# Stick-breaking softplus on whole tiles with its own table set, and the modulation product in 256-column blocks

## The reference, cut to what matters

```
log_1m = where(earlier, log_sigmoid(-z), 0)
between = cumsum(log_1m, reverse) - log_1m
att = where(earlier, exp(log_sigmoid(z) + between), 0)
```

```
mod = silu(c) @ w_ada + b_ada        # [1,1024] @ [1024,3072], twice
shift, scale, gate = split(mod, 3)
```

## Time and profile before

| | |
|---|---|
| median of 3 runs | 1934.13 us (1929.14 to 1935.0) |
| the profiled execution's own time | 1935.0 us |
| its span, first to last instruction | 1932.9 us |
| PE busy | 1817.4 us, 94% |
| DVE, ACT, POOL busy | 1263.3, 1029.7, 146.0 us |
| mean granted TensorE clock | 0.974 |
| HBM read | 284.06 MB |

### The profile page before, as it was taken

The page is one execution under the profiler, slowest core; times in us unless marked ns, Lnnn a source line. Parts: engine busy times, 40 slices in busy tenths (PEclk is TensorE's granted clock), DMA queues, the critical chain, the costliest instruction groups (busy, mean ns, idle before and its releaser), DMA issues.

```text
span 1932.9 us, 43768 instructions
## 1 busy us (share of the span) xinstructions
PE 1817.4 (94%) x18871; PEld 1631.5 (84%) x18871; DVE 1263.3 (65%) x1783; ACT 1029.7 (53%) x1585; POOL 146.0 (8%) x106
## 2 busy tenths in 40 slices
PE   6987999999989999898999999998899999998998
PEld 5887788889979888887698888887798888887887
DVE  6875367865436675486668856876467755775764
ACT  5834455554535554354655545744465554564455
POOL 0051100000000000014000000151100000000000
PEclk9999999999989999899899999999999999998999
DMA  6420145557576655355465562320245555443441
GB/s 190 132 86 4 53 146 184 190 182 244 174 233 217 197 191 180 110 174 178 150 198 184 186 204 93 120 76 4 68 153 191 178 188 169 134 146 104 152 132 66
DMA packets 288535, 287.92 MB, mean 149 GB/s; under 512 B 15240, under 2 KB 286456, under 8 KB 288344
## 3 DMA queue, kind: packets, MB, share of 16 engines
q1 hardware_dynamic: 285048, 284.02, 45.8%
q10 hardware_dynamic: 3296, 1.11, 0.3%
HBM read 284.06 MB, written 1.05 MB: 148 GB/s over the span
## 4 chain that ended last, share of the span: by engine, by line
PE 90%; DVE 4%; issue 3%; ACT 2%; DMA 0%; POOL 0%; SPq 0%; DVEq 0%; ACTq 0%; POOLq 0%
PE ps L419 23%; PE ps L420 12%; PE ps L401 10%; PE ps L403 9%; PE ps L402 9%; PE ps L814 3%; PE ps L436 2%; PE ps L437 2%; PE ps L438 2%; PE ps L713 1%; PE ps L784 1%; PE ps L798 1%; PE ps L675 1%; PE ps L641 1%; PE ps L727 1%
## 5 line engine op out<-in xcount | busy, mean ns | idle before, releaser
L463 DVE TENSOR_TENSOR wl<-raw,wh 128x1024 fp32r<-128x1024 f32 x484 | 596.5, 1251 | 345.4 <-ACT wh L453 340.9
L453 ACT ACTIVATE wh<-raw 128x1024 fp32r<-128x1024 f32 x484 | 499.4, 1041 | 432.0 <-PE ps L420 191.2
L419 PE MATMUL ps<-HH,wh 128*128 128x512 f32 x1408 | 489.7, 391 | 0.0
L420 PE MATMUL ps<-HH,wl 128*128 128x256 f32 x1408 | 397.0, 282 | 0.0
L419 PEld LDWEIGHTS ps<-HH,wh 128*128 128x128 f32 x1408 | 264.3, 188 | 55.6 <-issue 0.4
L401 PE MATMUL ps<-HH,wh 128*128 128x256 f32 x928 | 271.4, 292 | 10.2 <-DVE HH L2498 5.5
L420 PEld LDWEIGHTS ps<-HH,wl 128*128 128x128 f32 x1408 | 266.1, 189 | 0.1
L402 PE MATMUL ps<-HH,wh 128*128 128x256 f32 x928 | 263.6, 284 | 0.0
L403 PE MATMUL ps<-HH,wl 128*128 128x256 f32 x928 | 263.3, 284 | 0.0
L401 PEld LDWEIGHTS ps<-HH,wh 128*128 128x128 f32 x928 | 179.3, 193 | 20.8 <-issue 6.6
L402 PEld LDWEIGHTS ps<-HH,wh 128*128 128x128 f32 x928 | 179.6, 193 | 1.2 <-issue 1.2
(11 more groups left out here) (323 smaller groups left out, 3119.6 us busy)
## 6 DMA issues: line engine op xcount, KB each, us to landing
raw<-in_ffn_w_gu_dram SPq DMA_DIRECT2D x88, 1024.0 KB, 5.1
raw<-in_ffn_w_down_dram SPq DMA_DIRECT2D x32, 1024.0 KB, 5.1
raw<-in_w_in_dram SPq DMA_DIRECT2D x32, 1024.0 KB, 5.4
raw<-in_rw_w_rkv_dram SPq DMA_DIRECT2D x24, 1024.0 KB, 5.3
B<-in_w_ada_dram SPq DMA_DIRECT2D x24, 1024.0 KB, 7.7
raw<-in_ds_w_in_dram SPq DMA_DIRECT2D x14, 1024.0 KB, 5.3
raw<-in_ffn_w_down_dram SPq DMA_DIRECT2D x16, 768.0 KB, 4.4
raw<-in_sb_w_qkv_dram SPq DMA_DIRECT2D x12, 1024.0 KB, 5.5
```

The source lines that it names most:

```text
L419: e.matmul(o[:, m, :], h_[:, k, c], x_, start=k0 + k == 0, stop=False, skip_group_check=True)
L420: i = e.matmul(o[:, m, 0:S], l_[:, k, c], x_[:, 0, :], start=False, stop=k0 + k == kt - 1, skip_group_check=True)
L453: e.activation(wh[:, u % UNITS, 0:kn * 256], raw[:, j % RAW, k0 * 256:(k0 + kn) * 256], ACT.Copy).then_inc(*up("hi"))
L463: e.tensor_tensor(wl[:, u % UNITS, 0:kn * 256], raw[:, j % RAW, k0 * 256:(k0 + kn) * 256], wh[:, u % UNITS, 0:kn * 256].bitcast(F32), ALU. ...
```

## The change

Five things change.

1. `pe_ada` works block by block: 16 matmuls of 256 moving columns instead of 32 of 128; the eight k go to the four partition groups in turn, so the groups now hold partial sums over k. Each block signals its own end, and only its own load is waited for.
2. `act_ada` copies 128x512 instead of 128x128, and `pe_mod` adds the four groups and turns the result with four matmuls of one column instead of one of four.
3. On ACT, `softened` is cut in three: `sizes` (two Abs), `exps` (one Exp over 128x1536) and `logs` (a load of the table set `natural_log`, then one Ln over 128x1536). `weights` first loads the combined table set again. One `hi` now stands ahead of `sizes` and one between each of the parts. For g=3 `act_ada(2)` stands between `sizes` and `exps`.
4. On DVE, `soft(g)` stands behind q of the next group and one `lo`; it waits once for the single Ln.
5. In the feed-forward of layer 1, `dve_mod(6)` moves from i=7 to i=8.

```diff
-        add("sel", i[:, None] == 32 * np.arange(4)[None, :])
+        add("sel", (i % 32 == 0)[:, None])
...
         def pe_ada(e, t):
-            blocks = [2 * t, 2 * t + 1]
-            for i in blocks:
+            for u in range(2):
+                i = 2 * t + u
+                w = whole(KD, 256)(ada_slot[i])
                 e.wait_ge(s_ada[i % 4], 16 * (i // 4 + 1))
-            for k in range(KD):
-                for c in range(4):
-                    w = whole(KD, 256)(ada_slot[blocks[c // 2]])
-                    q = e.matmul(o[32 * c:32 * c + 32, 0:128], scb[:, k, :], w[:, k, c % 2 * P:c % 2 * P + P], ...)
-            q.then_inc(*up("mm", ("ada block", 2 * t), ("ada block", 2 * t + 1), ("ada", t)))
+                for k in range(KD):
+                    q = e.matmul(o[32 * (k % 4):32 * (k % 4) + 32, u * 256:u * 256 + 256], scb[:, k, :], w[:, k, :],
+                                 start=k < 4, stop=k >= 4, skip_group_check=True)
+                q.then_inc(*up("mm", ("ada block", i), *([("ada", t)] if u else [])))
...
         def pe_mod(e, t):
-            e.matmul(o[:, 0:4], ada_rows[:, 0:P], C("sel"), ...)
+            for m in range(4):
+                q = e.matmul(o[:, m:m + 1], ada_rows[:, m * P:m * P + P], C("sel"), ...)
...
         act_ada:
-            e.activation(ada_rows, PS("ada", t)[:, 0:P], ACT.Copy)
+            e.activation(ada_rows, PS("ada", t)[:, :], ACT.Copy)
...
         act_stickbreak:
-            def softened(g):    # 2 Abs, 2 Exp, 2 Ln of 128x768
+            def sizes(g):       # 2 Abs of 128x768
+            def exps(g):
+                e.activation(exw, exw, ACT.Exp, scale=-1.0)
+            def logs(g):
+                e.preload_act_table_set("natural_log")
+                e.activation(exw, exw, ACT.Ln, bias=1.0)
             def weights(g):
+                log_and_exp(e)
...
             for g in range(3):
-                softened(g)
-                hi(e)
+                hi(e, 1)
+                sizes(g)
+                hi(e, 1)
+                exps(g)
                 if g:
                     act_ada(e, g - 1)
-                hi(e)
+                hi(e, 1)
+                logs(g)
+                hi(e, 1)
                 weights(g)
                 hi(e)
-            softened(3)
+            sizes(3)
             act_ada(e, 2)
+            exps(3)
+            logs(3)
             act_ada(e, 3)
             act_ada(e, 4)
             weights(3)
...
         dve_ffn:
-                if layer == 1 and i == 7:
+                if layer == 1 and i == 8:
                     dve_mod(e, 6)
...
         dve_stickbreak:
             for g in range(3):
+                block("q", g + 1)
+                lo(e, 1)
                 soft(g)
-                block("q", g + 1)
+                lo(e, 1)
+                block("k", g + 1)
                 lo(e)
-                block("k", g + 1)
                 if g:
                     dve_mod(e, g - 1)
-                lo(e)
                 value_block(g + 1)
                 heads_out(g)
```

More of the change, by code:

```diff
@@ L517, in build @@
         ada_slot = [BUF[i] for i in (9, 10, 11, 9, 10, 11, 9, 10, 11, 2, 9, 10, 7, 9, 10, 7, 11, 14, 2, 11, 14, 2, 11, 14)]
-        ada_rows = BUF[12][:, 768:896]
+        ada_rows = BUF[12][:, 768:1280]
         def ada_load(e, i):
@@ L706, in pe_ada @@
                 e.wait_ge(*at("dve", "scb"))
-            blocks = [2 * t, 2 * t + 1]
-            for i in blocks:
+            for u in range(2):
+                i = 2 * t + u
+                w = whole(KD, 256)(ada_slot[i])
                 e.wait_ge(s_ada[i % 4], 16 * (i // 4 + 1))
-            for k in range(KD):
-                for c in range(4):
-                    w = whole(KD, 256)(ada_slot[blocks[c // 2]])
-                    q = e.matmul(o[32 * c:32 * c + 32, 0:128], scb[:, k, :], w[:, k, c % 2 * P:c % 2 * P + P],
-                                 start=k == 0, stop=k == KD - 1, skip_group_check=True)
-            q.then_inc(*up("mm", ("ada block", 2 * t), ("ada block", 2 * t + 1), ("ada", t)))
+                for k in range(KD):
+                    q = e.matmul(o[32 * (k % 4):32 * (k % 4) + 32, u * 256:u * 256 + 256], scb[:, k, :], w[:, k, :],
+                                 start=k < 4, stop=k >= 4, skip_group_check=True)
+                q.then_inc(*up("mm", ("ada block", i), *([("ada", t)] if u else [])))
         def pe_mod(e, t):
@@ L719, in pe_mod @@
             e.wait_ge(*at("act", ("ada", t)))
-            e.matmul(o[:, 0:4], ada_rows[:, 0:P], C("sel"), start=True, stop=True,
-                     skip_group_check=True).then_inc(*up("mm", ("mod", t)))
+            for m in range(4):
+                q = e.matmul(o[:, m:m + 1], ada_rows[:, m * P:m * P + P], C("sel"), start=True, stop=True, skip_group_check=True)
+            q.then_inc(*up("mm", ("mod", t)))
         def pe_to_tm(e, key, src, j):
@@ L1450, in act_ada @@
                 e.wait_ge(*at("mm", ("mod", t - 1)))
-            e.activation(ada_rows, PS("ada", t)[:, 0:P], ACT.Copy).then_inc(*up("act", ("ada", t)))
+            e.activation(ada_rows, PS("ada", t)[:, :], ACT.Copy).then_inc(*up("act", ("ada", t)))
         def act_ffn(e, layer):
@@ L1700, in act_stickbreak @@
             ex, at_ = sb_pairs(BUF[7]), sb_pairs(BUF[8])
-            def softened(g):
+            exw = BUF[7][:, 0:1536]
+            def sizes(g):
                 for r in range(2):
                     e.wait_ge(*at("mm", ("sb", "z", 2 * g + r)))
[L1705 to L1711, removed]
+                    i = e.activation(ex[r], PS2[r][:, :, 0:384], ACT.Abs)
+                i.then_inc(*up("act", ("sb", "abs", g)))
+            def exps(g):
+                e.wait_ge(*at("act", ("sb", "abs", g)))
+                e.activation(exw, exw, ACT.Exp, scale=-1.0).then_inc(*up("act", ("sb", "e", g)))
+            def logs(g):
+                e.preload_act_table_set("natural_log")
+                e.wait_ge(*at("act", ("sb", "e", g)))
+                e.activation(exw, exw, ACT.Ln, bias=1.0).then_inc(*up("act", ("sb", "l", g)))
             def weights(g):
+                log_and_exp(e)
                 for r in range(2):
@@ L2401, in soft @@
             def soft(g):
+                e.wait_ge(*at("act", ("sb", "l", g)))
                 for r in range(2):
-                    e.wait_ge(*at("act", ("sb", "l", 2 * g + r)))
                     e.scalar_tensor_tensor(out=sp_[r], in0=PS2[r][:, :, 0:384], scalar=0.0, in1=ex[r], op0=ALU.max,
```

## The result

The changed kernel takes 1954.39 us (median of 4 runs, 1952.05 to 1963.59) against 1934.57 before (4 runs). Over all runs of both kernels the ratio is 1.0136, 95% interval 1.0107 to 1.0165: 1.4% slower, or 26 us. Its 29 executions spread from 1950.6 to 1970.5. The profiled one took 1962.87, span 1960.7, mean clock 0.967. I had forecast slower by 17.6 (1943 to 1958); the direction held, the size did not: 1.0136 times 1934.1 is 1960.

What follows compares the result with a forecast made beforehand. PE was taken to bound the kernel, busy 94% of the span. The terms +7.1 +3.4 -3.5 +3.4 +4.8 +2.4 = +17.6 us on 1934.1 gave 1951.7 us, 0.9% slower, range 1943 to 1958.

Steps and rivals of the forecast that it cites:

- What bounds the kernel: Whole kernel: PE, busy 94% of the span; ACT and DVE work is free until PE waits for it.
- The waits before `sums`: Stick-breaking groups 0 to 2: PE waits 2.3, 2.4 and 2.4 us for ACT's longer chain, +7.1 us.
- the link named first: Stick-breaking groups on ACT: the `hi` ahead of `sizes` makes Abs run behind it, from 506.8 instead of 500.6.
- the rival that made it 1.4 longer: Stick-breaking table switch: each wait 1.4 longer, clock dropping every time; +23.5 us, 1957.6; chance 0.08.
- `pe_mod`: Modulation matmuls on PE: eight machine instructions at 0.07 us instead of two, +0.42 each; +3.4 outside the tail.
- `pe_ada`: Modulation matmuls on PE: half the instructions with twice the columns change nothing; 0, bounds -0.15 and +0.2 each.
- The tail: Stick-breaking stage's end: `act_ada(2)` comes earlier, so the output projection starts earlier; -3.5 us, longer `pe_mod` included.
- u(8): Feed-forward of layer 1: PE waits for the bank `dve_mod(6)` frees, +4.8 us, and +2.4 for the clock behind.
- The clock after the waits: Behind the three waits before `sums`: clock falls to half speed after two of three, +3.4 us, bounds 0 and 5.1.
- The sum: Whole kernel: all terms together +17.6 us on the median of 1934.1, giving 1951.7 us, 0.9% slower.

Runs made afterwards that it cites:

- experiment 9: Changed kernel with the first `hi` of each stick-breaking group moved from ahead of the Abs to behind the Exp; ratio to the kernel before 1.0142.
- 10: Changed kernel with each group's third `hi` moved behind `logs`, and `soft` ahead of both `lo` on DVE; ratio to the kernel before 1.0107.
- 3: Changed kernel without the eight table loads of the stick-breaking stage, Ln taken from the combined set; ratio to the kernel before 1.0066.
- experiment 5: Kernel before with only `pe_mod`'s one matmul of four columns split into four of one column; ratio to the kernel before 1.0045.
- experiment 6: Kernel before with the new `pe_ada`, `act_ada` and `pe_mod`, no order changed; ratio to the kernel before 1.0045.
- tail_only: Kernel before with `act_ada(2)` moved behind the two Abs of group 3, ahead of its Exp; ratio to the kernel before 0.9978.
- old_stick: Changed kernel with ACT's and DVE's order of the stick-breaking stage as in the kernel before, the rest changed; ratio to the kernel before 1.0088.
- ada_only: Same run as experiment 6: kernel before with the new `pe_ada`, `act_ada` and `pe_mod`, no order changed; ratio 1.0045.
- mod4: Same run as experiment 5: kernel before with only `pe_mod`'s matmul split into four of one column; ratio 1.0045.
- early_mod: Changed kernel with `dve_mod(g-1)` of the stick-breaking groups ahead of the two `lo` again; ratio to the kernel before 1.0113.
- third_behind: Same run as 10: changed kernel with each group's third `hi` behind `logs`, and `soft` ahead of both `lo`; ratio 1.0107.
- abs_first: Same run as experiment 9: changed kernel with each group's first `hi` moved behind the Exp; ratio 1.0142.
- experiment 1: Changed kernel with `dve_mod(6)` back at i=7 of the feed-forward; ratio to the kernel before 1.0095.
- experiment 8: The changed kernel measured once more, nothing altered, on the same chip as the other experiments; ratio to the kernel before 1.0145.

## Why the prediction was right in direction and short in size

- **What bounds the kernel.** Right for what the trace locates: it is waits of PE, instructions added to it, and PE at half clock.
- **The waits before `sums`.** Right in place and size: 3 x 2.20 = 6.6 for +7.1. Wrong in the link named first. I led the chain from the `hi` ahead of `sizes`; experiment 9 shows that it alone is innocent, and 10 and 3 that the third `hi` and the table load make the wait. My own sum had the third `hi`'s release in it, so the number came out right.
- **The table switch.** The load is 1.28 and the next ACTIVATE starts 1.30 after the load's start; the rival that made it 1.4 longer did not come, although its time, 1957.6, is the nearest to the result. The Trainium skill ("ScalarE: Activation LUTs", section "What ACT_TABLE_LOAD costs") adds a drain of about 1.38 us; no run here shows one: taking the load out shortened the waits by 1.42, of which 1.28 is the load. My text leaves most of this rival out of the range, yet its 1957.6 lies inside 1943 to 1958.
- **`values(2)`.** Missed. I told the move of `soft` on DVE but not that of `dve_mod(g-1)` behind two `lo`, the very rule that I applied to u(8): a bank is freed where its reader stands. 1.7 us.
- **`pe_mod`.** Mis-sized: +0.42 each by 0.07 per instruction, measured 0.67 in the trace, and 8.7/12 = 0.72 in time (experiment 5). With its own 128x128 weight load an instruction takes 0.10. At half clock it takes 0.22, so that a `pe_mod` costs 1.77 there against 0.49 for the pair of the kernel before. Over twelve, 3 to 4 us at full clock.
- **`pe_ada`.** Right: no gain from half the instructions (experiment 6).
- **The tail.** This is the step that failed. I took -3.5, bounds -2.3 and -4.6, with the longer `pe_mod` in it; the two profiles of the changed kernel show +1.2 and -0.6. The mechanism is there: the wait for `act_ada(2)` fell to 1.95 as forecast, `tail_only` gains 4 us, and against `old_stick` the new order gains 2.9 and 4.6. Mis-sized is what the new instructions cost there. In the old order they lengthen the tail from 22.1 to 26.0 (`ada_only`), 2.3 of it by the split `pe_mod` alone (`mod4`), where I had 4 x 0.42 = 1.7. And the clock decides: in the changed kernel it fell to half speed at about 569 and stayed until about 582.5, and a dearer `pe_mod` at half clock makes that stretch longer. Six profiles run this same tail; in three (`early_mod`, `third_behind`, `abs_first`: 18.6 to 19.5 us, against 22.1) the gain lies within my bounds, in three it doesn't.
- **u(8).** Right: 4.46 for 4.8, and it goes with the move (experiment 1). The half clock behind it cost 1.4 in both profiles, I had 2.4; in five other kernels with the same wait it cost 2.2 to 2.6.
- **The clock after the waits.** I took two falls of three, at 1.7 each. The first profile has one, the second three, and over five profiles it is 13 of 15 (experiment 8). `scores(3)` ends 4.8 later in the second profile than in the first, while the waits ahead of it are the same; this fits the wide spread of the kernel's runs.
- **Behind the last change.** Missed. My sum has nothing for the stretch where the code is the same, and gives no reason for it. It took 4.7 and 8.0 us longer than in the kernel before.
- **The sum.** By the first profile, against the forecast: the tail +4.7, the stretch behind the change +4.7, `pe_mod` outside the tail +2.2, `values(2)` +1.7; less 0.5 for the waits, 1.7 for the clock behind them and 1.3 for u(8). From 17.6 this leads to 27.4, of 27.9. All my upper bounds together (8.0 + 5.1 - 2.3 + 5.0 + 4.8 + 4.3) come to 24.9 and would not have held the 26 either. The misses have both signs, so that the sum is nearer to the result than its terms are.

What stays open: why the clock held behind two of fifteen waits of 2.20 us, what in the stretch behind the change makes it 971 us in some kernels and 975 to 979 in others, and how much of the tail's gain is left beside the dearer `pe_mod`.

## What to carry to other kernels

- When an instruction is moved behind others on one engine, list every buffer it frees, not only what it waits for: here a 0.15 us addition moved by one step of a loop held TensorE for 4.46 us, and another for 1.74.
- An in-order engine that is half idle is not free: what counts is the chain behind the last release it waits for. Move one link at a time on the chip before naming the one that binds.
- Where the bound engine's clock depends on its idle time, a short wait may cost itself and nearly as much again (here 2.20 and 1.7), and not in every execution; it may also fall in code that did not change. Judge such a change by many runs, and read the clock in each profile.

## What was not expected of the hardware

- A one-column matmul in float32 with a weight load of its own takes 0.10 us per machine instruction at full clock and 0.22 at half: splitting one four-column matmul in four took 0.81 instead of 0.14 (8.7 us over twelve).
- After an idle time of TensorE of 2.20 us before `sums` the granted clock fell to half in 13 of 15 cases, in five profiles; after 0.78 to 1.26 us in the same place in none of nine.
- After an idle time of 1.99 us at one place it fell in all twelve profiles of kernels with eight small `pe_mod` matmul instructions ahead of it, and in none of the four with two: the length of the idle time alone does not tell.
- Sixteen matmuls of 256 columns, in four groups of 32 columns of the array, take 1.93 us, 32 of 128 columns 1.95, and 3.64 both at half clock: the price goes by the columns.
